# S5 tiles and state space heads in pairs, each of a pair in its own group of the array, and the first phases of S5 made at once

## The chip, the core and the metric

The kernel runs on one core of a Trainium2 chip. The metric is the time of one execution on the device in microseconds (us); lower is better. The core's engines are TensorE (PE), VectorE (DVE), ScalarE (ACT), GpSimd (POOL) and SyncE (SP), which issues the DMAs.

## The reference

Two blocks of layers run over one sequence of 256 positions with 2048 features, in f32. The change touches two pieces of them. The first is the state space layer (`ssd_scan`), with 64 heads of 64 columns in 8 groups and two chunks of 128 positions:

```python
decay = jnp.exp(jnp.where(causal, da_t[..., :, None] - da_t[..., None, :], -jnp.inf))
cb = jnp.einsum('bclgn,bcsgn->bcgls', cm, bm)
y_diag = jnp.einsum('bcgls,bcgels,bcsgep->bclgep', cb, decay, xdt)
```

The second is the S5 branch, a complex linear recurrence with 64 groups of 64 states, 16 inputs and 16 outputs each:

```python
x_r = jnp.einsum('bsgc,gpc->bsgp', ug, bb_r)
x_i = jnp.einsum('bsgc,gpc->bsgp', ug, bb_i)
_, _, h_r, h_i = lax.associative_scan(_complex_affine_combine, (a_seq_r, a_seq_i, x_r, x_i), axis=1)
y = (jnp.einsum('bsgp,gcp->bsgc', h_r, c_re) - jnp.einsum('bsgp,gcp->bsgc', h_i, c_im))
y = y + d_skip.reshape(N_SSM_GROUPS, SSM_GROUP) * ug
z = jax.nn.gelu(y.reshape(bsz, seq, D_SSM)) @ w_glu
```

Around them stand projections, an LRU and an mLSTM layer, gated linear attention, differential attention, gates and a feed-forward layer. Nearly all of the arithmetic is in products with 550 MB of weights.

## The kernel before

**The main stream.** All weight blocks of 128x128 come in a fixed order, eight to a unit, 1010 units. SP loads a unit into one of 7 RAW buffers (L2005), ACT copies it rounded into WH (L901), DVE forms the rest WL = RAW - WH (L1329), and PE makes three fp32r matmuls with each block: high and low weights by the high part of x, high weights by the low part. In most stages a matmul has 256 columns. WH has 5 buffers, so ACT waits for PE's last use of a unit, and the pace of all engines is PE's.

**The steps.** Everything else runs in chains of numbered steps beside the stream. `walk` goes through the plan on every engine alike: after each unit it runs one step of every open chain. So a step takes one unit, and the order of instructions in each engine's queue is written by the step numbers: what PE is to use at step r must be made by DVE or POOL in an earlier one, or PE stands in front of it with the main stream queued behind. `STEPS` holds the number of steps of each chain.

**State space heads.** In each group g of eight heads, `ssd(g, s)` has ACT make the decay DB of one head at each step 1 to 8 (L1089 ff.; it reads a row of running sums that a DMA has spread into CSB), DVE mask it at steps 2 to 9 (name "msk"), and PE multiply it at steps 3 to 10: two f32 products per head (256 and 128 columns, 64 weight columns XDT), into rows 0 to 63 of a bank for an even head and 64 to 127 for an odd one. DB has 3 buffers.

**S5.** 128 states (two groups) are a tile; there are 32 tiles. `s5_tiles` gives tile n the steps r = s - (11 + 11 (n // 2) + 5 (n % 2)), so two tiles take 11 steps. At r = 0 PE forms Bu (BR, BI: 32 rows of the array, by the tile's place n % 4), at 1 ACT copies it to BX and, swapped, to BS; at 2 DVE multiplies BX by the cosine table and POOL BS by the sine table (name "bsm"); at 3 DVE adds them, runs two scans into BS and multiplies by the cosine into HH, and POOL multiplies by the sine into BX ("bss"); at 5 DVE joins HH; at 6 PE forms y with CR and CI (32 columns of the array, by n % 4, into bank 7). BX has two buffers, BS and HH one. The odd tile's y stands in the same step as the even Bu of the next pair.

**Phases.** The tables TB (cosine and sine of the phase at 256 positions, two tiles a table, two tables) are made by POOL in `phases(b, r)` at steps 11 b + r, r = 0 to 8: each step doubles the length filled so far (for 64 positions and more by 64 at a time) in six operations, after the tile's own operations of the same step. The S5 chain runs beside the projections for gated attention (`gla`, `dec`), differential attention (`diff`) and the branch outputs (`g12`, `gb`, `db`). Its last steps apply GELU and split the result into ZS (`rest`); `End("s5")` runs what is left of it after the first tile of `g0`.

## Time and profile before

| | us |
|---|---|
| median of 3 runs | 3366.08 |
| lowest, highest | 3359.88, 3367.69 |
| the profiled execution | 3367.36 |
| its span in the trace | 3365.6 |
| PE busy, DVE busy | 3195.7, 2287.2 |
| ACT busy, POOL busy | 1841.0, 674.8 |

The page shows one execution. A matmul's record is longer than its share of PE's time, since matmuls overlap; the distance from start to start tells what one costs, and the idle time before an instruction what was waited for. [...]

### The profile page before, as it was taken

How to read it: one execution, taken by the hardware profiler on the slowest of the kernel's cores; microseconds unless marked ns; L12 is line 12 of the kernel's file. 1: busy time of each engine (PE TensorE's matmuls, PEld its weight loads, DVE VectorE, ACT ScalarE, POOL GpSimd, SP SyncE). 2: the span in 40 equal slices, each digit the busy share in tenths (PEclk: the TensorE clock that was granted, in tenths of full speed). 3: DMA queues.
4: the chain of work that ended last, by engine and by line, in shares of the span. 5: the costliest groups of instructions: out<-in, count | busy, mean ns of one | idle time of the engine just before them, and what ended most of it. 6: DMA issues, size and time to landing. Idle time of an engine off the chain costs nothing.

```text
span 3365.6 us, 54085 instructions
## 1 busy us (share of the span) xinstructions
PE 3195.7 (95%) x21726; PEld 2917.0 (87%) x21726; DVE 2287.2 (68%) x3156; ACT 1841.0 (55%) x2371; POOL 674.8 (20%) x1110
## 2 busy tenths in 40 slices
PE   6989898999999999998999998989999999999998
PEld 6889888889999999887887887888998888888887
DVE  6655788656778777656656676666566788888554
ACT  5544778545666666553555544333545666666443
POOL 1000000000000000114656777774001000000000
PEclk9999999999999999999999999889999999999999
DMA  5445444555455555555333433434555555555554
GB/s 195 145 132 178 137 149 153 195 191 197 169 170 174 170 171 191 179 180 192 132 113 117 134 126 127 137 126 146 205 183 187 188 191 191 188 192 190 188 191 140
DMA packets 158045, 560.53 MB, mean 167 GB/s; under 512 B 17552, under 2 KB 25808, under 8 KB 157152
## 3 DMA queue, kind: packets, MB, share of 16 engines
q1 hardware_dynamic: 157792, 557.06, 49.3%
q8 instruction: 170, 2.79, 0.3%
q14 instruction: 83, 0.68, 0.1%
HBM read 550.64 MB, written 6.36 MB: 165 GB/s over the span
## 4 chain that ended last, share of the span: by engine, by line
PE 70%; DVE 11%; POOL 8%; ACT 7%; issue 3%; DMA 1%; SPq 0%; DVEq 0%; ACTq 0%; POOLq 0%
PE ps L561 70%; POOL TB L1917 4%; DVE WL L1329 3%; ACT WH L901 2%; ACT L891 2%; POOL PT L1917 2%; POOL BX L1917 1%; POOL BS L1917 1%; DVE HH L1292 1%; DVE X L1303 0%; DMA scratch<-X 0%; DVE BS L1319 0%; DVE XC L1303 0%; DVE XV L1303 0%; DVE XC L1319 0%
## 5 line engine op out<-in xcount | busy, mean ns | idle before, releaser
L561 PE MATMUL ps<-XN,WH 128*128 128x256 f32 (+1 forms) x8864 | 1876.7, 305 | 47.6 <-DVE WL L1329 25.7
L901 ACT ACTIVATE WH<-RAW 128x1024 fp32r<-128x1024 f32 x1010 | 1065.5, 1057 | 1266.7 <-PE ps L561 1232.8
L1329 DVE TENSOR_TENSOR WL<-RAW,WH 128x1024 fp32r<-128x1024 f32 x1010 | 1262.5, 1256 | 499.4 <-ACT WH L901 492.8
L561 PEld LDWEIGHTS ps<-XN,WH 128*128 128x128 f32 x8864 | 1447.6, 194 | 137.8 <-DVE WL L1329 28.5
L561 PE MATMUL ps<-XN,WL 128*128 128x256 f32 x5120 | 1453.8, 284 | 0.0
L561 PEld LDWEIGHTS ps<-XN,WL 128*128 128x128 f32 x5120 | 989.0, 193 | 0.0
L561 PE MATMUL ps<-YS,WH 128*128 128x512 f32 (+1 forms) x1088 | 369.9, 388 | 4.7 <-DVE YS L1292 2.2
L1917 POOL TENSOR_TENSOR RSB<-RSB,SQ 128x256 f32<-128x256 f32 x75 | 75.0, 1000 | 1212.4 <-ACT SQ L891 1211.2
L561 PE MATMUL ps<-YS,WL 128*128 128x256 f32 x1056 | 296.5, 281 | 0.0
L561 PEld LDWEIGHTS ps<-YS,WH 128*128 128x128 f32 x1088 | 202.8, 189 | 49.0 <-DVE YS L1292 2.5
L1917 POOL TENSOR_TENSOR SQ<-SQ 128x512 f32<-128x512 f32 (+1 forms) x24 | 33.1, 1378 | 1052.5 <-ACT SQ L891 1051.5
L561 PE MATMUL ps<-HS,WH 128*128 128x512 f32 x688 | 238.6, 392 | 0.0
L891 ACT ACT_TABLE_LOAD x154 | 197.6, 1283 | 8.7 <-PE ps L561 1.7
L561 PEld LDWEIGHTS ps<-YS,WL 128*128 128x128 f32 x1056 | 199.4, 189 | 0.0
L561 PE MATMUL ps<-HS,WL 128*128 128x256 f32 x688 | 192.7, 280 | 0.0
L561 PEld LDWEIGHTS ps<-HS,WH 128*128 128x128 f32 x688 | 129.2, 188 | 28.5
L1917 POOL TENSOR_TENSOR TB<-TB,PW 128x128 f32<-128x128 f32 (+6 forms) x288 | 148.7, 516 | 22.6
L1917 POOL TENSOR_TENSOR PT<-TB,PW 128x128 f32<-128x128 f32 (+6 forms) x288 | 144.1, 500 | 22.6
L1917 POOL TENSOR_TENSOR TB<-TB,PT 128x128 f32<-128x128 f32 (+6 forms) x288 | 140.7, 489 | 22.6
L561 PEld LDWEIGHTS ps<-HS,WL 128*128 128x128 f32 x688 | 129.3, 188 | 0.0
L561 PE MATMUL ps<-ZS,WH 128*128 128x256 f32 x512 | 91.0, 280 | 3.0 <-DVE ZS L1292 3.0
L1292 DVE TENSOR_TENSOR X<-X,ps 128x256 f32<-128x256 f32 x128 | 53.9, 421 | 56.5 <-PE ps L561 53.1
(328 smaller groups left out, 3438.1 us busy)
## 6 DMA issues: line engine op xcount, KB each, us to landing
RAW<-in_w SPq DMA_DIRECT2D x1010, 512.0 KB, 3.3
CSB<-sums SPq DMA_DIRECT2D x64, 128.0 KB, 3.7
scratch<-X SPq DMA_DIRECT2D x2, 2048.0 KB, 7.9
X<-scratch SPq DMA_DIRECT2D x2, 2048.0 KB, 7.8
X<-in_x SPq DMA_DIRECT2D x4, 512.0 KB, 7.6
X<-in_x SPq DMA_DIRECT2D x1, 2048.0 KB, 9.2
out<-X SPq DMA_DIRECT2D x4, 512.0 KB, 2.6
WIF<-in_w_if SPq DMA_DIRECT2D x1, 576.0 KB, 14.4
```

The lines of the kernel that those rows point to most:

```text
L561: return pe.e.matmul(dst, l, r, start=start, stop=stop, skip_group_check=True)
L891: act.e.activation(dst, src, f, bias=bias, scale=scale).then_inc(*act.one(*names))
L901: act.e.activation(WH[:, w % NH, :], RAW[:, w % NB, :], ACT.Copy).then_inc(*act.one(("wh", w)))
L1292: dve.e.tensor_tensor(dst, a, b, op).then_inc(*dve.one(*names))
L1329: dve.e.tensor_tensor(WL[:, w % NB, :], RAW[:, w % NB, :], WH[:, w % NH, :].bitcast(F32), SUB).then_inc(*dve.one(("wl", w)))
L1917: pool.e.tensor_tensor(dst, a, b, op).then_inc(*pool.one(*names))
```

## The change

- State space heads: PE takes two heads at steps 4, 6, 8 and 10 instead of one at each step 3 to 10. The two 256-column products come first, one for each half of the array's columns, then the two with 128. DB has 4 buffers for 3; CSB 4 for 5; RS3 is dropped for RS1.
- S5: `s5_pairs` runs both tiles of a pair together, a pair every 10 steps, and the chain has 178 steps for 197. PE forms Bu of both at r = 0 (into two banks) and y of both at r = 10, each alternating between the two tiles; ACT copies at 1 and 2; DVE's and POOL's operations for even and odd tile stand at neighbouring steps (see the diff). BS has two buffers, and the joined result stays in BS, without HH.
- Phases: POOL makes the first 16 positions of all 32 tiles at once at steps 0 to 3 (`rotate` on PB), and then a pair's table from a copy and four doublings, the last with 128 new positions at once.

```diff
-NCSB = 5
+NCSB = 4
...
-    "dv": 1, "dq": 1, "diff": 15, "g12": 1, "gb": 1, "db": 1, "g0": 1, "gg": 1, "gl": 2, "s5": 197, "wo": 1,
+    "dv": 1, "dq": 1, "diff": 15, "g12": 1, "gb": 1, "db": 1, "g0": 1, "gg": 1, "gl": 2, "s5": 178, "wo": 1,
...
-        DB = [m(f"DB{i}", 384) for i in range(3)]
+        DB = [m(f"DB{i}", 384) for i in range(4)]
         YB = v3(m("YB", 1024), 4)
-        RS3 = m("RS3", 256)
...
-        BS = v3(m("BS", 512), 2)
-        HH = v3(m("HH", 512), 2)
-        PT = m("PT", 2 * 64)
+        BS = [v3(m(f"BS{i}", 512), 2) for i in range(2)]
+        PT = m("PT", 256)
...
+        PB = m("PB", 2 * 32 * 16).rearrange("p (c n a) -> p c n a", c=2, n=32)
...
-                if 3 <= s <= 10:
-                    e_ = s - 3
+                if s in (4, 6, 8, 10):
+                    e_ = s - 4
                     if e_ % 4 == 0:
                         take("side", "yb", g, e_ // 4)
                         kept.add(holder_of("yb", g, e_ // 4))
                     b = PS[holder_of("yb", g, e_ // 4)]
-                    c, r, d = 256 * ((e_ % 4) // 2), 64 * (e_ % 2), DB[e_ % 3]
-                    pe.wait_ge(*at("msk", g, e_))
-                    mm(b[r:r + 64, c:c + 256], XDT[:, 0, 64 * e_:64 * e_ + 64], d[:, 0:256], True, False)
-                    mm(b[r:r + 64, c + 128:c + 256], XDT[:, 1, 64 * e_:64 * e_ + 64], d[:, 256:384], False,
-                       True).then_inc(*pe.one(("ymm", g, e_)))
+                    c = 256 * ((e_ % 4) // 2)
+                    pe.wait_ge(*at("msk", g, e_ + 1))
+                    two = [(64 * i, DB[(e_ + i) % 4], slice(64 * (e_ + i), 64 * (e_ + i) + 64)) for i in range(2)]
+                    for q, d, x in two:
+                        mm(b[q:q + 64, c:c + 256], XDT[:, 0, x], d[:, 0:256], True, False)
+                    for q, d, x in two:
+                        i = mm(b[q:q + 64, c + 128:c + 256], XDT[:, 1, x], d[:, 256:384], False, True)
+                    i.then_inc(*pe.one(("ymm", g, e_), ("ymm", g, e_ + 1)))
...
-                for n, r in s5_tiles(s):
-                    ft, q_ = n // 4, n % 4
-                    rows = slice(32 * q_, 32 * q_ + 32)
+                for m, r in s5_pairs(s):
+                    ft = m // 2
+                    pair = [(n, slice(32 * (n % 4), 32 * (n % 4) + 32)) for n in (2 * m, 2 * m + 1)]
                     if r == 0:
-                        b = take("side", "bu", n)
+                        b = [take("side", "bu", n) for n, _ in pair]
                         pe.wait_ge(*at("us", ft))
                         pe.wait_ge(*at("b1"))
                         pe.wait_ge(*at("b2"))
-                        mm(b[:, 0:256], BR[rows, ft, :], US[rows, ft, :])
-                        mm(b[:, 256:512], BI[rows, ft, :], US[rows, ft, :]).then_inc(*pe.one(("bu", n)))
-                    if r == 6:
-                        if q_ == 0:
+                        for c, src in ((slice(0, 256), BR), (slice(256, 512), BI)):
+                            for i, (n, rows) in enumerate(pair):
+                                x = mm(b[i][:, c], src[rows, ft, :], US[rows, ft, :])
+                        x.then_inc(*pe.one(("bu", 2 * m), ("bu", 2 * m + 1)))
+                    if r == 10:
+                        if m % 2 == 0:
                             take("y", "sy", ft)
                         b = PS[holder_of("sy", ft)]
-                        pe.wait_ge(*at("hh", n))
+                        pe.wait_ge(*at("hh", 2 * m + 1))
                         pe.wait_ge(*at("cc"))
-                        mm(b[rows, 0:256], CR[:, n, :], HH[:, 0, :], True, False)
-                        mm(b[rows, 0:256], CI[:, n, :], HH[:, 1, :], False, True).then_inc(*pe.one(("sy", n)))
+                        for c, src in enumerate((CR, CI)):
+                            for n, rows in pair:
+                                x = mm(b[rows, 0:256], src[:, n, :], BS[n % 2][:, c, :], c == 0, c == 1)
+                        x.then_inc(*pe.one(("sy", 2 * m), ("sy", 2 * m + 1)))
...
-                for n, r in s5_tiles(s):
-                    if r == 1:
-                        b = bank("bu", n)
+                for m, r in s5_pairs(s):
+                    if r in (1, 2):
+                        n = 2 * m + r - 1
+                        b, i = bank("bu", n), n % 2
                         act.wait_ge(*at("bu", n))
                         if n > 1:
-                            act.wait_ge(*at("hh", n - 2))
-                        if n:
-                            act.wait_ge(*at("hhc", n - 1))
-                            act.wait_ge(*at("bss", n - 1))
-                        fn(BX[n % 2], v3(b, 2), ACT.Copy)
-                        fn(BS[:, 0, :], b[:, 256:512], ACT.Copy)
-                        fn(BS[:, 1, :], b[:, 0:256], ACT.Copy, ("bx", n), ("free", "bu", n), scale=-1.0)
-                if s == 192:
+                            act.wait_ge(*at("sy", n - 2))
+                        fn(BX[i], v3(b, 2), ACT.Copy)
+                        fn(BS[i][:, 0, :], b[:, 256:512], ACT.Copy)
+                        fn(BS[i][:, 1, :], b[:, 0:256], ACT.Copy, ("bx", n), ("free", "bu", n), scale=-1.0)
...
-                for n, r in s5_tiles(s):
-                    ft, q_ = n // 4, n % 4
-                    tb = TB[:, (n // 2) % 2]
-                    cc, ss = tb[:, 0, n % 2, :], tb[:, 1, n % 2, :]
-                    c2 = cc.unsqueeze(1).to_broadcast([128, 2, 256])
-                    b = BX[n % 2]
-                    if r == 2:
+                for m, r in s5_pairs(s):
+                    n = 2 * m + {2: 0, 3: 1, 4: 0, 5: 1, 7: 0, 8: 1}.get(r, 0)
+                    x, y = BX[n % 2], BS[n % 2]
+                    c2 = TB[:, m % 2, 0, n % 2, :].unsqueeze(1).to_broadcast([128, 2, 256])
+                    if r in (2, 3):
                         dve.wait_ge(*at("bx", n))
-                        dve.wait_ge(*at("tb", n // 2))
-                        tt(b, b, c2, MUL)
-                    if r == 3:
+                        dve.wait_ge(*at("tb", m))
+                        tt(x, x, c2, MUL)
+                    if r in (4, 5):
                         dve.wait_ge(*at("bsm", n))
-                        tt(b, b, BS, ADD)
+                        tt(x, x, y, ADD)
                         mg = MAG[:, n:n + 1].to_broadcast([128, 256])
                         for c in range(2):
-                            scan(BS[:, c, :], mg, b[:, c, :], 0.0, MUL, ADD, ("scn", n))
-                        if n:
-                            dve.wait_ge(*at("sy", n - 1))
-                        tt(HH, BS, c2, MUL, ("hhc", n))
-                    if r == 5:
+                            scan(y[:, c, :], mg, x[:, c, :], 0.0, MUL, ADD, ("scn", n))
+                    if r in (7, 8):
                         dve.wait_ge(*at("bss", n))
-                        tt(HH[:, 0, :], HH[:, 0, :], b[:, 0, :], SUB)
-                        tt(HH[:, 1, :], HH[:, 1, :], b[:, 1, :], ADD, ("hh", n))
-                    if r == 7 and q_ == 3:
-                        dve.wait_ge(*at("sy", n))
+                        tt(y, y, c2, MUL, ("hhc", n))
+                        tt(y[:, 0, :], y[:, 0, :], x[:, 0, :], SUB)
+                        tt(y[:, 1, :], y[:, 1, :], x[:, 1, :], ADD, ("hh", n))
+                    if r == 12 and m % 2:
+                        ft = m // 2
+                        dve.wait_ge(*at("sy", 2 * m + 1))
...
+            def rotate(tb, n, l, tiles, *names):
+
+                d = 1 << l
+                c, s_ = [PW[:, i, l, tiles].unsqueeze(2).to_broadcast([128, n, d]) for i in range(2)]
+                t = PT[:, 0:n * d].rearrange("p (n a) -> p n a", n=n)
+                x, y = slice(0, d), slice(d, 2 * d)
+                tt(tb[:, 0, :, y], tb[:, 0, :, x], c, MUL)
+                tt(t, tb[:, 1, :, x], s_, MUL)
+                tt(tb[:, 0, :, y], tb[:, 0, :, y], t, SUB)
+                tt(tb[:, 1, :, y], tb[:, 0, :, x], s_, MUL)
+                tt(t, tb[:, 1, :, x], c, MUL)
+                tt(tb[:, 1, :, y], tb[:, 1, :, y], t, ADD, *names)
...
+                    fill(PB[:, 0, :, 0:1], 1.0)
+                    fill(PB[:, 1, :, 0:1], 0.0)
+                if s < 4:
+                    rotate(PB, 32, s, slice(0, 32))
+                m, r = divmod(s - 4, 10)
+                if s >= 4 and m < 16 and r in (0, 1, 2, 4):
+                    tb = TB[:, m % 2]
+                    if r == 0:
+                        if m > 1:
+                            pool.wait_ge(*at("hhc", 2 * m - 3))
+                        pool.wait_ge(*pool.last)
+                        pool.e.tensor_copy(tb[:, :, :, 0:16], PB[:, :, 2 * m:2 * m + 2, :]).then_inc(*pool.one())
+                    rotate(tb, 2, {0: 4, 1: 5, 2: 6, 4: 7}[r], slice(2 * m, 2 * m + 2), ("tb", m))
+                for m, r in s5_pairs(s):
+                    n = 2 * m + {2: 0, 3: 1, 5: 0, 6: 1}.get(r, 0)
+                    x, y = BX[n % 2], BS[n % 2]
+                    ss = TB[:, m % 2, 1, n % 2, :]
+                    if r in (2, 3):
                         pool.wait_ge(*at("bx", n))
-                        tt(BS, BS, ss.unsqueeze(1).to_broadcast([128, 2, 256]), MUL, ("bsm", n))
-                    if r == 3:
+                        tt(y, y, ss.unsqueeze(1).to_broadcast([128, 2, 256]), MUL, ("bsm", n))
+                    if r in (5, 6):
                         pool.wait_ge(*at("scn", n))
-                        tt(b[:, 0, :], BS[:, 1, :], ss, MUL)
-                        tt(b[:, 1, :], BS[:, 0, :], ss, MUL, ("bss", n))
-                b, r = divmod(s, 11)
-                if b < 16 and r < 9:
-                    phases(b, r)
+                        tt(x[:, 0, :], y[:, 1, :], ss, MUL)
+                        tt(x[:, 1, :], y[:, 0, :], ss, MUL, ("bss", n))
...
+def s5_pairs(s):
+
+    return [(m, s - 9 - 10 * m) for m in range(16) if 0 <= s - 9 - 10 * m < 13]
```

On PE in the first group of heads the names are ps (bank), DB (decay of a head), XDT (weights of a head), XN, WH and WL (the main stream). Before, one unit of the main stream (cut here) stands between two heads:

```order
L561 MATMUL ps1<-XN_52,WL_50 128x256
L561 MATMUL ps5<-DB0_121,XDT_119 64x256
L561 MATMUL ps5<-DB0_121,XDT_119 64x128
L561 MATMUL ps2<-XN_52,WH_51 128x256 x2
...
L561 MATMUL ps2<-XN_52,WL_50 128x256
L561 MATMUL ps5<-DB1_122,XDT_119 64x256
L561 MATMUL ps5<-DB1_122,XDT_119 64x128
```

After, at the second of these two places:

```order
L560 MATMUL ps2<-XN_52,WL_50 128x256
L560 MATMUL ps5<-DB0_121,XDT_119 64x256
L560 MATMUL ps5<-DB1_122,XDT_119 64x256
L560 MATMUL ps5<-DB0_121,XDT_119 64x128
L560 MATMUL ps5<-DB1_122,XDT_119 64x128
```

The first head's products moved behind the unit that followed them, and the two heads alternate.

On PE in the later part of S5 (HH, or BS after, is the state; CR and CI form y in bank 7; US, BR and BI form Bu), before, at the step that holds the odd y and the next even Bu:

```order
L561 MATMUL ps7<-HH_162,CR_156 32x256
L561 MATMUL ps7<-HH_162,CI_157 32x256
L561 MATMUL ps6<-US_158,BR_154 128x256
L561 MATMUL ps6<-US_158,BI_155 128x256
```

After, where y of a pair and Bu of the next meet:

```order
L560 MATMUL ps7<-BS0_160,CR_155 32x256
L560 MATMUL ps7<-BS1_161,CR_155 32x256
L560 MATMUL ps7<-BS0_160,CI_156 32x256
L560 MATMUL ps7<-BS1_161,CI_156 32x256
L560 MATMUL ps6<-US_157,BR_153 128x256
L560 MATMUL ps3<-US_157,BR_153 128x256
L560 MATMUL ps6<-US_157,BI_154 128x256
L560 MATMUL ps3<-US_157,BI_154 128x256
```

All eight products of a pair's steps stand together; the two other places of S5 per pair are gone from PE.

On POOL in the same part (BS<-BS,TB is "bsm", BX<-BS,TB "bss", the rest phases), before, for an odd tile:

```order
L1917 TENSOR_TENSOR BS<-BS,TB 128x512
L1917 TENSOR_TENSOR TB<-TB,PW 128x2x64
L1917 TENSOR_TENSOR PT<-TB,PW 128x128
L1917 TENSOR_TENSOR TB<-TB,PT 128x2x64
L1917 TENSOR_TENSOR TB<-TB,PW 128x2x64
L1917 TENSOR_TENSOR PT<-TB,PW 128x128
L1917 TENSOR_TENSOR TB<-TB,PT 128x2x64
L1917 TENSOR_TENSOR BX_160<-BS,TB 128x256 x2
```

After, for both tiles of a pair:

```order
L1915 TENSOR_TENSOR BS_160<-BS_160,TB 128x512
L1915 TENSOR_TENSOR BS_161<-BS_161,TB 128x512
L1975 COPY TB<-PB 128x4x16
L1915 TENSOR_TENSOR TB<-TB,PW 128x2x16
...
L1915 TENSOR_TENSOR BX_158<-BS_160,TB 128x256 x2
L1915 TENSOR_TENSOR TB<-TB,PW 128x2x32
...
L1915 TENSOR_TENSOR BX_159<-BS_161,TB 128x256 x2
L1915 TENSOR_TENSOR TB<-TB,PW 128x2x64
```

The widest phases moved behind the last of a pair's products; six of 128x2x16 and six of 128x2x32 (or their PT form) stand before the even and the odd BX.

## Rows read from the trace of the kernel before

**Rows 1.** Page: the span, and PE's busy us, share and instructions.

```profile
span 3365.6 us, 54085 instructions
PE 3195.7 (95%) x21726; PEld 2917.0 (87%) x21726; DVE 2287.2 (68%) x3156; ACT 1841.0 (55%) x2371; POOL 674.8 (20%) x1110
```

**Rows 2.** Windows: stretch, length, busy us by engine, then PEclk, DMA share, GB/s.

```profile
820.00:1340.00 520.00, 517.45 (x3974) 483.69 (x3974) 392.32 (x557) 347.49 (x442) 19.30 (x14) 1.00 0.52 174
1600.00:2040.00 440.00, 406.35 (x2614) 358.89 (x2612) 293.98 (x419) 227.16 (x325) 301.40 (x557) 0.94 0.37 123
2040.00:2318.00 278.00, 252.75 (x1798) 231.65 (x1798) 175.91 (x218) 100.34 (x122) 208.54 (x362) 0.90 0.40 133
2600.00:3100.00 500.00, 500.00 (x2886) 437.31 (x2885) 405.75 (x612) 317.13 (x445) 6.64 (x7) 1.00 0.57 190
```

**Rows 3.** PE's waits, 2040 to 2318: releaser, us, times, longest.

```profile
PE ps L561 <- DVE HH L1292: 25.2, 6, 5.1
```

**Rows 4.** PE's waits, 1600 to 2040.

```profile
PE ps L561 <- DVE HH L1292: 14.8, 8, 4.2
PE ps L561 <- ACT RS L891: 6.6, 2, 4.1
```

**Rows 5.** Timeline of PE at a late y: start, us, instruction, idle before.

```profile
2121.04 0.62 PE L561 MATMUL ps<-HH,CR 128*32 128x256 f32 x2 [3.78 <-DVE HH L1292]
...
2124.45 0.41 PE L561 MATMUL ps<-DOS,WL 128*128 128x256 f32 x1
```

**Rows 6.** Timeline of POOL before that y.

```profile
2111.02 1.29 POOL L1917 TENSOR_TENSOR BS<-BS,TB 128x512 f32<-128x512 f32 x1
...
2115.73 1.26 POOL L1917 TENSOR_TENSOR PT<-TB,PW 128x128 f32<-128x128 f32 x1
2117.07 0.45 POOL L1917 TENSOR_TENSOR TB<-TB,PT 128x128 f32<-128x128 f32 x1
2117.66 2.32 POOL L1917 TENSOR_TENSOR BX<-BS,TB 128x256 f32<-128x256 f32 x2
```

**Rows 7.** Windows: one pair of S5 tiles, from Bu to Bu.

```profile
2140.51:2184.66 44.15, 40.43 (x282) 36.81 (x281) 28.28 (x36) 15.44 (x19) 34.70 (x63) 0.88 0.40 132
```

**Rows 8.** Groups of POOL, 1590 to 2345: count, busy us, mean ns, idle before.

```profile
L1917 POOL TENSOR_TENSOR BX<-BS,TB 128x256 f32<-128x256 f32 x64 | 72.9, 1139 | 54.0 <-DVE BS L1319 48.8
L1917 POOL TENSOR_TENSOR PT<-TB,PW 128x128 f32<-128x128 f32 x90 | 63.0, 699 | 7.1
...
L1917 POOL TENSOR_TENSOR TB<-TB,PW 128x64 f32<-128x64 f32 x30 | 14.6, 487 | 2.3
```

**Rows 9.** Timeline of PE around an undisturbed Bu, then y.

```profile
2097.48 0.28 PE L561 MATMUL ps<-XN,WL 128*128 128x256 f32 x1
...
2098.74 0.50 PE L561 MATMUL ps<-XN,WH 128*128 128x256 f32 x2
...
2101.60 0.28 PE L561 MATMUL ps<-XN,WL 128*128 128x256 f32 x1
2101.81 0.62 PE L561 MATMUL ps<-HH,CR 128*32 128x256 f32 x2
2102.26 0.59 PE L561 MATMUL ps<-HH,CI 128*32 128x256 f32 x2
2102.79 0.50 PE L561 MATMUL ps<-XN,WH 128*128 128x256 f32 x2
```

**Rows 10.** Timeline of PE: before the second head of a group, and the sixth.

```profile
834.07 0.28 PE L561 MATMUL ps<-XN,WL 128*128 128x256 f32 x1
...
849.49 0.28 PE L561 MATMUL ps<-XN,WL 128*128 128x256 f32 x1
850.13 0.86 PE L561 MATMUL ps<-DB,XDT 128*64 128x256 f32 x4 [0.36 <-DVE DB L1292]
```

**Rows 11.** PE's waits, 815 to 1345.

```profile
PE ps L561 <- DVE DB L1292: 2.5, 7, 0.4
```

**Rows 12.** Page: the costliest groups, the first products of ZS.

```profile
L561 PE MATMUL ps<-ZS,WH 128*128 128x256 f32 x512 | 91.0, 280 | 3.0 <-DVE ZS L1292 3.0
```

57 lines of the change are left out of this document (11 added, 46 removed).

## The prediction

> **What bounds the kernel now.** I read five views in this order. The page gives the span and TensorE (PE) at 95% busy [rows 1], so only PE's own work, PE's waits and PE's clock can move the time. The windows by stage then part the span [rows 2]. The state space stage (820 to 1340 us) has a granted clock of 1.00 and PE busy 517.45 of 520 us: PE alone bounds it. The feed-forward stage is PE-bound too, with VectorE (DVE) at 405.75 of 500 us, so a DVE share of 81% does not by itself hold PE up. The S5 stretch is different. [...] The list of PE's waits names one cause for the second part: six waits for the tile HH from DVE, 25.2 us [rows 3]. In the first part the same wait has 14.8 us, next to others [rows 4].
>
> The timeline shows what the wait is. Of each pair of S5 tiles the odd one is late: PE stands 3.78 us before the HH product, and the matmuls behind it are slow: one of 128x256 takes 0.41 us [rows 5] where it takes 0.28 at full clock [rows 9]. [...] The late part comes to 25.2 us of waits and (1 - 0.90) x 278 = 27.8 us of clock, together 53.0.
>
> Who is late is in GpSimd's (POOL's) timeline [rows 6]: the product BS (step 2 of a tile) begins at 2111.02, DVE's sum waits for it, and between it and the products BX (step 3) stand six phase operations, 2112.39 to 2117.5, one of them 1.26 us. BX begins at 2117.66, and HH follows only at 2120. POOL was busy 34.70 of 44.15 us in the next pair's window, with some 0.08 us between operations (63 x 0.08 = 5): 39.7 of 44.15 [rows 7]. It is nearly full, in an order that puts phases ahead of what PE waits for.
>
> **The change, part by part.**
>
> 1. POOL's phases. Before, each pair costs 54 phase operations. After, the first sixteen phases of all 32 tiles are made once (24 operations and two fills), and a pair costs one copy and 24 operations of 128x32, 128x64, 128x128 and 128x256. By the means of the S5 stretch [rows 8]: the twelve narrow ones at the 0.49 us of a 128x64, 5.9; six of 128x128 at 0.69, 4.1; six of 128x256, a shape the phases do not have now, bounded by the 1.14 of BX (6.8) and by two 128x128 (8.3), and I take 6.8, the same shape; two BS at the 1.29 of [rows 6], 2.6; four BX at 1.14, 4.6; the copy 0.5. That is 24.5, with 31 gaps of 0.08 27.0 us a pair. The table made at once is about 6 x (0.49 + 0.49 + 0.69 + 1.14) = 16.9 us, before the first tile needs POOL, where POOL now makes 54 operations for the first pair: nothing.
>
> 2. The steps. A pair now takes 10 units of eight blocks instead of 11, BS has two steps before DVE's sum instead of one, and HH two between DVE and PE instead of one (DVE at steps 7 and 8, PE at 10). The odd BS is followed by copy and six 128x32 and then the even BX, so what stands ahead of a waited-for product is 3.4 us instead of the 5.1 from 2112.39 to 2117.5. PE's own time for 10 units: a unit is 24 matmuls 0.12 apart, 2.87 us, so 28.7 plus the packed products below, 31.5. POOL needs 27.0 of it, DVE 28.28 of 44.15 now [rows 7], about 26.8 with one unit less: 85%, a little over the feed-forward's 81%. Everything fits, PE is the longest, and what is late next is the odd HH again, by the least slack. I leave 1 us per pair for it in the six late pairs (6 us) and count the rest as won: 53.0 - 6 = **47 us**. Bounds: 26 (half stays) to 53.
>
> 3. The early part (1600 to 2040). [...] But PE also waits there for ACT and DVE in chains of gated attention and differential attention [rows 4], which start at PE's own products; a PE that comes earlier waits longer there, and S5's steps, moved by up to 19 units, now meet other steps in the queues of ACT and DVE. Bounds 0 and 32 us. I take the lower end, **0**.
>
> 4. Products in different groups of the array. Each f32 product is two halves on PE, 0.22 us apart for 256 columns (2101.81 to 2102.26 holds two) [rows 9]. A group of four halves costs start to start, less one ordinary 0.12, 1.14 us for Bu and 1.07 for y [rows 9], and 0.1 more on leaving, since the second matmul after it is late. For a state space head four units take 849.49 - 834.07 = 15.42 us, 3.86 each [rows 10]: 0.99 above 2.87. No row shows two products in different groups one behind the other, so this is bounded from both sides. One after another, only a lead-in per pair goes: four halves more cost 0.88, so Bu 2.12 against 2 x 1.24, y 2.05 against 2 x 1.17, heads 1.65 against 2 x 0.99; 0.65 x 16 + 0.33 x 32 = 21 us. Entirely side by side: half of all, (1.24 + 1.17) x 16 + 0.99 x 32 = 70 us. The order of issue lies between: the two halves of one product share a group, and PE starts in order, so only the second half of one and the first of the next can overlap, at three borders of seven. That gives Bu 2.12 - 0.66 = 1.46, y 1.39, heads 1.65 - 0.44 = 1.21 (the borders at 128 columns are half as wide): **31.5 us** in S5 and (1.98 - 1.21) x 32 = 24.6 in the heads. A dearer exchange of groups (0.1 at each of three borders, 64 pairs) would take 19 us off the 21 of the lower bound.
>
> [...]
>
> 5. The heads' own waits. One head of a group is late today: PE idles 0.36 us at 850.13 [rows 10], seven times, 2.5 us in all [rows 11]. It is the sixth. Now PE comes to it without the fifth's 0.99 us, whose product is moved behind the same wait, so it waits 0.99 longer: 7 x 0.99 = 6.9. ACT's copies have four buffers for three, CSB four for five; a row lands long before its use. The heads give 24.6 - 6.9 = **17.7 us** (bounds 4 and 25).
>
> 6. The end. S5 is done 19 units before the gated sums need ZS, and that wait of **3.0 us** goes [rows 12].
>
> Two side banks are taken at once for Bu where one was; ACT frees them in the next two steps, before the four of the ring come round, and I count nothing.
>
> Sum: 47 + 0 + 31.5 + 17.7 + 3.0 = 99 us. The profiled execution took 3367.4 us (span 3365.6), so 3268; the median of the runs is 1.3 lower. I forecast **3267 us**.
>
> **The rivals.**
> - No overlap of groups at all: the products give 21 instead of 56, so 3267 + 35 = 3302 us. For it: no row shows overlap. Chance 0.13.
> - Rows overlap, columns don't: y loses 0.66 x 16 = 10.6 and the heads 0.44 x 32 = 14, 3292 us. Chance 0.10.
> - The early part gives all its 32 us too: 3235 us. For it: four of its waits look exactly like the late ones. Against: the other waits in rows 4. Chance 0.11.
> - POOL and DVE hold each other up more than the means say, and half of the late stalls with their slow clock stay: 3267 + 26 = 3293 us. For it: a 128x128 product of POOL took 1.26 us beside DVE's split and 0.45 without [rows 6], and DVE's share rises to 85%. [...] Chance 0.10.
> - **Slower.** The same mechanism in full: each of POOL's 31 operations a pair waits for one of DVE's, as the 1.26 did, now that wide ones replace the narrow. At 1.40 us each the pair takes 46 us. S5 then takes 16 x 46 + 18 x 2.87 = 788 us, where it takes 741 now (1600 to 2341); less 20.7 for heads and end that is +26: 3392 us. It turns at 44.4 us a pair, against 27.0 by the means. Chance 0.03.
> - The pairs do nothing: the stall moves whole to the new waiting place, and groups do not overlap: of the 21 us and the 3 of ZS the heads' wait takes 6.9 and a dearer exchange of groups some 10: 3359 us. Chance 0.03.
>
> **How the numbers follow.** The forecast has 0.50, and its own range is 3250 to 3285. From 3235 to 3302 all rivals but the last two lie, 0.94 by the cases; full overlap alone lies at 3253, together with the early part at 3221. I widen only upward, to 3310, for clock and waits that none of the cases names. A difference under 0.3% (10 us) can't be told from no change in this kernel. Faster by more than that: all but the last two cases, 0.94; within it 0.03; slower 0.03.
>
> **What the profile after would show.** Step 2: PE's wait for its y product under 10 us in all and the granted clock of the last S5 pairs near 1.00, a pair every 31 to 33 us. Step 1: POOL busy some 25 us a pair. Step 3: new waits of PE for ACT or DVE in the attention part, as long as those of HH that went. Step 4: the starts of eight halves in one group, 1.4 us from first to leaving instead of 2. Step 5: a wait of 1.3 us at the third pair of heads of each group. The prediction is wrong if POOL's operations lengthen beside DVE, or if the eight halves start 0.22 apart.

## The result

| kernel | median of the runs, us | lowest to highest | profiled span, us |
|---|---|---|---|
| before | 3366.89 | 3359.88 to 3369.28 | 3365.6 |
| after | 3268.49 | 3265.13 to 3270.49 | 3268.7 |

The ratio is 0.971, with a 95% interval of 0.9698 to 0.9722: 98.4 us less. The forecast was 3267 us, so the sum came out within 2 us. Two of its terms did not: the products of S5 were 6 us too small, and the gain of the heads was about twice too large. The rest of this text takes them apart.

The page after begins with these two lines. They answer to [rows 1]: PE does the same 21726 instructions in 87 us less busy time, and POOL has 640 operations where it had 1110.

```profile
span 3268.7 us, 53596 instructions
PE 3108.3 (95%) x21726; PEld 2873.6 (88%) x21726; DVE 2313.3 (71%) x3156; ACT 1837.6 (56%) x2371; POOL 541.3 (17%) x640
```

The windows after, over the stretches of [rows 2] (stretch, length, busy us by engine, then PEclk, DMA share, GB/s). The stretches are the same times from the start, not the same work, since after runs ahead by then.

```profile
820.00:1340.00 520.00, 501.26 (x4005) 480.83 (x4004) 394.29 (x559) 348.16 (x444) 22.40 (x16) 0.98 0.55 176
...
1600.00:2040.00 440.00, 407.64 (x2836) 372.85 (x2835) 346.36 (x462) 238.73 (x341) 261.52 (x338) 0.95 0.40 133
2040.00:2318.00 278.00, 275.01 (x2299) 269.57 (x2298) 209.70 (x252) 129.61 (x151) 119.95 (x134) 1.00 0.55 182
```

PEclk is the mean granted clock of the stretch, as a share of full speed. The traces of all kernels here record two levels of it, 1.00 and 0.50, and the mean of a stretch with both lies between. Behind the late product of [rows 5] it is 0.50 from 2123 to 2129 us, and there the matmuls of 128x256 start 0.21 us apart (2124.66 to 2124.87), where they start 0.12 apart at 1.00 (832.43 to 832.55 in after).

Three readings. The late S5 stretch went from a granted clock of 0.90 to 1.00, and PE is busy 275 of 278 us there. The early stretch hardly moved, 0.94 to 0.95. And the state space stage, which was at 1.00 and full, is now at 0.98 and PE is idle for 19 of 520 us. That last row is the surprise of the profile: the change made PE's products there shorter, and PE began to wait.

PE's waits after, late stretch (2040 to 2260), then the state space stage (820 to 1345). They answer to [rows 3] and [rows 11].

```profile
PE ps L560 <- DVE BS L1293: 3.0, 3, 1.3
```

```profile
PE ps L560 <- DVE DB L1293: 18.7, 15, 2.3
```

The wait for HH (now in place, in BS) is 3.0 us instead of 25.2. The wait for DB is 18.7 us instead of 2.5.

PE's timeline where both products of two S5 tiles follow each other (x4 is four halves, two products), then at a pair of heads (x8 is eight halves). Records overlap: that of a matmul of the main stream is 0.28 us long, with 0.12 us from its start to the next, so starts are compared.

```profile
2067.51 0.28 PE L560 MATMUL ps<-XN,WL 128*128 128x256 f32 x1
2067.72 0.63 PE L560 MATMUL ps<-BS,CR 128*32 128x256 f32 x4
2068.17 0.60 PE L560 MATMUL ps<-BS,CI 128*32 128x256 f32 x4
2068.70 0.70 PE L560 MATMUL ps<-US,BR 32*128 32x256 f32 x4
2069.24 0.60 PE L560 MATMUL ps<-US,BI 32*128 32x256 f32 x4
2069.77 0.50 PE L560 MATMUL ps<-GOS,WH 128*128 128x256 f32 x2
```

```profile
832.76 0.87 PE L560 MATMUL ps<-DB,XDT 128*64 128x256 f32 x8
833.56 0.50 PE L560 MATMUL ps<-XN,WH 128*128 128x256 f32 x2
```

In [rows 9] two halves of CR took 0.45 us from start to start (2101.81 to 2102.26). Here four of them do (2067.72 to 2068.17). Two halves of BR took 0.54 in before (2097.69 to 2098.22), and four do here (2068.70 to 2069.24). The head product took 0.86 with four halves [rows 10], and eight take 0.87. The second member of each pair adds 0.01 us at most, in products that differ in rows (Bu) and in products that differ in columns (y, heads).

### The profile page after: what moved, and what is told of

It reads as the page before. It is cut to its first block, busy times and chain, and to the rows that moved or that the text cites. A ratio compares the mean times of both kernels' runs of the same rounds, so it can differ in the third digit from the quotient of the medians.

```text
span 3268.7 us, 53596 instructions
## 1 busy us (share of the span) xinstructions
PE 3108.3 (95%) x21726; PEld 2873.6 (88%) x21726; DVE 2313.3 (71%) x3156; ACT 1837.6 (56%) x2371; POOL 541.3 (17%) x640
## 4 chain that ended last, share of the span: by engine, by line
PE 75%; DVE 11%; ACT 8%; issue 2%; POOL 1%; DMA 1%; SPq 0%; DVEq 0%; ACTq 0%; POOLq 0%
PE ps L560 75%; DVE WL L1330 3%; ACT WH L907 2%; ACT L897 2%; DVE XV L1304 1%; DVE BS L1293 1%; POOL TB L1915 1%; DMA scratch<-X 0%; DVE X L1304 0%; ACT DB L897 0%; DVE BS L1320 0%; DVE XC L1304 0%; DVE XMC L1304 0%; DMA RAW<-in_w 0%; ACT RB L897 0%
## 5 line engine op out<-in xcount | busy, mean ns | idle before, releaser
L1915 POOL TENSOR_TENSOR TB<-TB,PT 128x32 f32<-128x32 f32 (+3 forms) x128 | 99.6, 778 | 10.0
L1304 DVE SCALAR_TENSOR_TENSOR VG<-UP,CV,VG 128x256 f32<-128x256 f32 x172 | 83.3, 484 | 12.6 <-DVE HS L1293 0.5
L560 PE MATMUL ps<-MS,WH 128*128 128x512 f32 x256 | 88.9, 392 | 0.9 <-DVE DVT L1293 0.9
```

What stands on the lines that cost most here:

```text
L560: return pe.e.matmul(dst, l, r, start=start, stop=stop, skip_group_check=True)
L1304: dve.e.scalar_tensor_tensor(out=dst, in0=a, scalar=s, in1=b, op0=o0, op1=o1).then_inc(*dve.one(*names))
L1915: pool.e.tensor_tensor(dst, a, b, op).then_inc(*pool.one(*names))
```

## The experiments

All times are medians. Each kernel was run in turn with the kernel before, whose median was 3368.07 in the first series, 3368.01 in the second and 3366.23 in the last.

| kernel | us | ratio to before, 95% interval |
|---|---|---|
| e1_heads_only | 3359.81 | 0.9971 (0.9962 to 0.9981) |
| e2_same_group | 3301.94 | 0.9802 (0.9787 to 0.9817) |
| e3_one_by_one | 3268.50 | 0.9703 (0.9690 to 0.9717) |
| e4_silu_late | 3247.43 | 0.9642 (0.9629 to 0.9655) |
| e5_short_phases | 3310.43 | 0.9828 (0.9815 to 0.9842) |
| e6_long_phases | 3310.44 | 0.9829 (0.9816 to 0.9843) |
| e7_unit_later | 3241.99 | 0.9628 (0.9614 to 0.9641) |
| e8_before_silu_late | 3365.31 | 0.9987 (0.9978 to 0.9996) |
| e9_s5_only | 3278.81 | 0.9736 (0.9720 to 0.9753) |

### Do different groups overlap, and does the order count?

**e2_same_group.** The kernel after, with the same number and size of matmuls, but both members of a pair in one group.

```diff
-                    c = 256 * ((e_ % 4) // 2)
...
-                    two = [(64 * i, DB[(e_ + i) % 4], slice(64 * (e_ + i), 64 * (e_ + i) + 64)) for i in range(2)]
-                    for q, d, x in two:
+                    q = 64 * ((e_ % 4) // 2)
+                    two = [(256 * i, DB[(e_ + i) % 4], slice(64 * (e_ + i), 64 * (e_ + i) + 64)) for i in range(2)]
+                    for c, d, x in two:
...
-                                x = mm(b[i][:, c], src[rows, ft, :], US[rows, ft, :])
+                                x = mm(b[i][:, c], src[pair[0][1], ft, :], US[pair[0][1], ft, :])
...
-                                x = mm(b[rows, 0:256], src[:, n, :], BS[n % 2][:, c, :], c == 0, c == 1)
+                                x = mm(b[pair[0][1], 256 * (n % 2):256 * (n % 2) + 256], src[:, n, :], BS[n % 2][:, c, :], c == 0, c == 1)
```

It computes something else: the products of the odd tiles and of half of the heads are left out or misplaced, so only its time says something.

> The kernel after, with both members of a pair in the same group of the array: Bu of an odd tile takes the rows of the even one, y of both lands in the even tile's partitions in two column ranges, and two heads of a pair land in the same 64 partitions in two column ranges (so the odd tiles' products are left out or misplaced; number, size and order of the matmuls are the same). If different groups are what overlaps, eight halves take 0.88 us more in Bu and in y (the 0.22 per half of the rows before): 0.88 x 2 x 16 = 28 us in S5, and 0.44 to 0.66 per pair of heads, which mostly shortens a wait that is there anyway: 3292 to 3305. If the saving came from packing eight halves behind one wait (one lead-in instead of two) and not from the groups, the time stays within 5 us of 3268.

Measured: 3301.94 us, 33.4 more than after. PE's timeline in it, at the same two places:

```profile
2061.40 1.05 PE L560 MATMUL ps<-BS,CR 128*32 128x256 f32 x4
2062.28 1.03 PE L560 MATMUL ps<-BS,CI 128*32 128x256 f32 x4
2063.24 1.13 PE L560 MATMUL ps<-US,BR 32*128 32x256 f32 x4
2064.21 1.02 PE L560 MATMUL ps<-US,BI 32*128 32x256 f32 x4
2065.16 0.50 PE L560 MATMUL ps<-DOS,WH 128*128 128x256 f32 x2
```

```profile
834.25 1.51 PE L560 MATMUL ps<-DB,XDT 128*64 128x256 f32 x8
835.70 0.51 PE L560 MATMUL ps<-XN,WH 128*128 128x256 f32 x2
```

From the first CR to the matmul behind BI it is now 3.76 us, and 2.05 in after (2067.72 to 2069.77): 1.71 more, x 16 pairs = 27.4 us. The four rows grow nearly alike, by 0.43, 0.43, 0.43 and 0.42 from start to start, so rows and columns overlap equally well. The groups are what overlaps; that the pair shares one wait and one lead-in is not enough. The other 6 us fit the heads: by the two rows a pair costs 0.64 more (1.51 for 0.87), 20 us for 32 pairs, while the stage's granted clock is 1.00 instead of 0.98 (10.5 us less) and its waits are 4.9 us shorter, 13.8 instead of 18.7:

```profile
PE ps L560 <- DVE DB L1293: 13.8, 14, 1.7
```

**e3_one_by_one.** The kernel after, with all products of the first tile or head issued ahead of those of the second.

```diff
-                        for c, src in enumerate((CR, CI)):
-                            for n, rows in pair:
+                        for n, rows in pair:
+                            for c, src in enumerate((CR, CI)):
```

and likewise for Bu and the heads.

> The kernel after, with the pair's products issued one tile (or head) after the other, all of the first and then all of the second, instead of alternating. By the prediction's step 4 only the second half of one product and the first of the next can overlap, so now one border of seven is left where three were: 0.44 us more for each eight halves against the step's own value, and against the full overlap that the trace shows 0.66 more in Bu and y, 0.66 x 32 = 21 us in S5, 3285 to 3292 (the heads' part hides in their wait). If PE starts products of another group ahead of the queue, whatever the order, nothing changes: 3264 to 3272.

Measured: 3268.50 us, the time of after to 0.01 us. Its timeline of PE:

```profile
2067.79 0.63 PE L560 MATMUL ps<-BS,CR 128*32 128x256 f32 x4
2068.25 0.61 PE L560 MATMUL ps<-BS,CI 128*32 128x256 f32 x4
2068.78 0.71 PE L560 MATMUL ps<-US,BR 32*128 32x256 f32 x4
```

The program has CR, CI of one tile and then CR, CI of the other. The trace has all four halves of CR start first. So the second tile's first product starts beside the first tile's, ahead of a product that stands before it in the queue. By the start times of the single halves it begins 13 ns after the first tile's (2067.790 and 2067.803); in after, where it stands next in the queue, 7 ns (2067.717 and 2067.724). The prediction's rule (PE starts in order, so only borders between neighbours overlap) was its author's estimate. In [rows 9] CR, CI and WH do start in the order of the queue, at 2101.81, 2102.26 and 2102.79, but no row has two products in different groups. The rule falls with this run: within such a group of eight halves the order does not count.

### Where did the heads' gain go?

**e1_heads_only.** The kernel before, with the heads' part of the change alone.

```diff
-NCSB = 5
+NCSB = 4
...
-        DB = [m(f"DB{i}", 384) for i in range(3)]
+        DB = [m(f"DB{i}", 384) for i in range(4)]
...
-                if 3 <= s <= 10:
-                    e_ = s - 3
+                if s in (4, 6, 8, 10):
+                    e_ = s - 4
```

> The kernel before with the heads' part of the change alone: heads two by two, four buffers DB and CSB, nothing of S5. The prediction on record says 17.7 us less than before (24.6 from the products, 6.9 lost in a new wait), 3349. What the two traces say together: by the last group of the state space stage the changed kernel is only 2.4 us ahead and by the end of the output projection about 7, so this part should give 3 to 8 us, 3359 to 3364, with waits for DB near 19 us in all and a granted clock of about 0.97 in the stage. A third view, that the heads' part pays but S5's steps took it back, would give 15 us or more here.

Measured: 3359.81 us, 8.3 less than before (6 to 13 by the interval). It waits as after does, in 820 to 1345:

```profile
PE ps L560 <- DVE DB L1292: 18.8, 15, 2.3
```

So the loss belongs to this part of the change, not to S5. The chain is in after's timeline of ACT at the middle of a group's heads (columns: start, us, instruction, idle before):

```profile
837.93 1.28 ACT L897 ACT_TABLE_LOAD   x1
839.22 1.06 ACT L897 ACTIVATE ZB<-ZB 128x1024 f32<-128x1024 f32 x1
840.37 0.95 ACT L897 ACTIVATE DB<-CSB,CST 128x256 f32<-128x256 f32 x2
841.34 1.28 ACT L897 ACT_TABLE_LOAD   x1
842.63 0.52 ACT L897 ACTIVATE DB<-DB 128x384 f32<-128x384 f32 x1
```

then DVE's and PE's:

```profile
843.19 0.56 DVE L1293 TENSOR_TENSOR DB<-DB,CBm 128x384 f32<-128x384 f32 x1 [4.08 <-ACT DB L897]
...
848.01 0.56 DVE L1293 TENSOR_TENSOR DB<-DB,CBm 128x384 f32<-128x384 f32 x1
```

```profile
848.62 1.55 PE L560 MATMUL ps<-DB,XDT 128*64 128x256 f32 x8 [2.31 <-DVE DB L1293]
...
850.69 0.41 PE L560 MATMUL ps<-XN,WL 128*128 128x256 f32 x1
```

ACT changes its table for the Silu of the z tiles and changes back for the next exponential: 1.28 + 1.06 + 1.28 us in the middle of the heads. DVE stands 4.08 us for it. By the time it has done that mask, a split, a row of the next group's convolution and the next mask, PE has waited 2.31 us for the sixth head, and runs the eight halves in 1.55 instead of 0.87 and the matmuls behind them at 0.41 instead of 0.28: the granted clock is 0.50 from 849 to 851 us.

**e4_silu_late.** The kernel after, with that Silu behind the last head.

```diff
-            def zs(g, j, s):
-                if j == 3:
-                    act.wait_ge(*at("zsr", g))
-                    fn(ZB, ZB, ACT.Silu, ("zsd_", g))
...
                     fn(d, d, ACT.Exp, ("dec_", g, e_), scale=-1.0)
+                if s == 9:
+                    act.wait_ge(*at("zsr", g))
+                    fn(ZB, ZB, ACT.Silu, ("zsd_", g))
```

> The kernel after, with ACT's Silu of the four z tiles moved from the middle of a group's heads (step of the fourth z tile) to step 9 of the group, behind the last head's exponential. Reading of the trace: that Silu with two loads of tables, 1.28 us each, is what makes the fifth and sixth heads' DB late, so PE waits about 2.6 us per group and then runs some 2 us worth of time at 1.2 GHz; without it the waits for DB fall from 18.7 to under 5 us, the granted clock of the stage to 1.00, and the time by 7 x 4.5 = 31 us, to 3235 to 3245. The rival: what is late is DVE, which has a row of the next group's convolution (4 operations, 2.4 us) between two masks; then the Silu gives only what ACT saves, under 8 us, 3260 or more.

Measured: 3247.43 us, 21.1 less than after. The waits and the window of 820 to 1345:

```profile
PE ps L560 <- DVE DB L1291: 4.5, 14, 0.3
```

```profile
820.00:1345.00 525.00, 518.37 (x4153) 495.37 (x4153) 414.09 (x584) 359.22 (x462) 29.07 (x22) 1.00 0.58 184
```

The waits shrink by 14.2 us and the clock returns to 1.00, which is worth about 0.02 x 525 = 10.5 us; together 24.7. The expectation of 31 multiplied the worst group by seven; the total of the list of waits, with the clock, comes within 4 us of what was measured. No run shows the clock in GHz that the expectation names; what after shows in that spell is the granted clock of 0.50. That the Silu in the middle makes PE wait is shown, and the rival (DVE's convolution row alone is late) is out.

**e8_before_silu_late.** The same edit of the Silu, made in the kernel before.

> The kernel before, with the Silu of the z tiles moved behind the last head alone. There PE waits only 2.5 us in all for the heads and its clock in the stage is 1.00, so by the reading of the traces this gives 2.5 us or less, 3364 to 3368: the Silu in the middle of the heads costs nothing until PE's products are shorter. If it gives 10 us or more, the gain of e4_silu_late had nothing to do with the change.

Measured: 3365.31 us, 2.7 less than before (1 to 7 by the interval), and the list of waits for DB is empty. The Silu in the middle cost about 3 us while the products were long, and 21 once they were short.

**e9_s5_only.** The kernel after without the heads' part.

```diff
-                if s in (4, 6, 8, 10):
-                    e_ = s - 4
+                if 3 <= s <= 10:
+                    e_ = s - 3
```

> The kernel after, with the heads' part taken back: heads one by one, three DB and five CSB, everything of S5 as changed. The heads' part alone gave 8 us (e1_heads_only); if the two parts do not touch each other this one has the rest, 3268.5 + 8 = 3276 us, within 3 us, with a granted clock of 1.00 in the state space stage. By the prediction on record it would be 3267 + 17.7 = 3285.

Measured: 3278.81 us, 87.4 less than its before, 10.3 more than after, with a clock of 1.00 in the stage:

```profile
820.00:1345.00 525.00, 522.45 (x4008) 488.18 (x4007) 395.13 (x559) 349.08 (x444) 22.36 (x16) 1.00 0.52 175
```

The two parts add up within the intervals: 87.4 + 8.3 = 95.7 against 98.4.

### Phases or steps?

**e5_short_phases.** The kernel before, its steps and single tiles untouched, with the phases of the change.

```diff
-                b, r = divmod(s, 11)
-                if b < 16 and r < 9:
-                    phases(b, r)
+                if s == 0:
+                    ...
+                    for l in range(4):
+                        rotate(PB, 32, l, slice(0, 32))
+                b, r = divmod(s, 11)
+                if b < 16 and r in (0, 1, 2, 4):
+                    ...
+                    rotate(tb, 2, {0: 4, 1: 5, 2: 6, 4: 7}[r], slice(2 * b, 2 * b + 2), ("tb", b))
```

> The kernel before, with GpSimd's phases of the change alone: the first sixteen phases of all tiles made once, then a copy and four doublings per pair of tiles (steps 0, 1, 2 and 4 of eleven). Tiles one by one, their steps and the heads stay as before. If the load and the order of GpSimd's queue were the cause of the late HH (step 1 of the prediction), the waits for HH in the late stretch fall from 25.2 to under 8 us, the granted clock there from 0.90 to 0.97 or more, and the time by 40 to 50 us, to 3318 to 3328. If the missing slack was in the steps (one step between BS, the sum, BX and HH), phases alone give half or less: 3340 or more.

Measured: 3310.43 us, 57.6 less than before. Its waits of PE from 2040 to 2290, and the windows of one late pair of tiles and of both stretches:

```profile
PE ps L562 <- DVE HH L1293: 2.7, 4, 0.9
```

```profile
2129.77:2165.89 36.12, 36.12 (x283) 33.69 (x281) 29.25 (x36) 15.68 (x19) 25.73 (x31) 1.00 0.50 162
1600.00:2040.00 440.00, 414.82 (x2764) 370.24 (x2763) 321.74 (x436) 237.64 (x338) 220.62 (x289) 0.97 0.40 130
2040.00:2290.00 250.00, 247.27 (x1928) 230.87 (x1927) 196.58 (x235) 105.92 (x128) 148.33 (x170) 1.00 0.49 159
```

The late stalls are gone with the old steps, so GpSimd's phases were their cause. Two things changed in its queue at once, the load and the order: no phase stands any more between the odd tile's BS and its BX, where [rows 6] had six.

```profile
2154.51 1.56 POOL L1918 TENSOR_TENSOR BS<-BS,TB 128x512 f32<-128x512 f32 x1
2160.38 2.93 POOL L1918 TENSOR_TENSOR BX<-BS,TB 128x256 f32<-128x256 f32 x2 [4.31 <-DVE BS L1320]
```

Which of the two would have been enough is not shown; no kernel was timed with all the phases and only their order changed. The early stretch improves too, from a clock of 0.94 to 0.97 and from 14.8 to 10.1 us of waits for HH (0.03 x 440 = 13 and 4.7 us), which covers what came beyond the 40 to 50 us expected.

**e6_long_phases.** The kernel after, with eight doublings per pair.

```diff
-                m, r = divmod(s - 4, 10)
-                if s >= 4 and m < 16 and r in (0, 1, 2, 4):
+                m, r = divmod(s - 2, 10)
+                if s >= 2 and m < 16 and r < 8:
...
-                    rotate(tb, 2, {0: 4, 1: 5, 2: 6, 4: 7}[r], slice(2 * m, 2 * m + 2), ("tb", m))
+                    rotate(tb, 2, r, slice(2 * m, 2 * m + 2), ("tb", m))
```

> The kernel after, with the phases of each pair made from the start again, by eight doublings in eight steps (48 operations and two fills per pair instead of 24 and a copy); pairs, steps and heads stay as changed. By the load: the pair of after has 26.9 us of GpSimd's work and some 2.6 of gaps; 24 narrow operations at 0.49 + 0.08 add 13.7, so about 43 us a pair against the 30.9 that PE takes. Then GpSimd bounds the late pairs, 8 to 16 of them by 12 us: 3365 to 3460. If the steps and pairs alone removed the stalls, the time stays under 3290.

Measured: 3310.44 us, 42.0 more than after, neither of the two expectations. PE's waits from 2040 to 2330 and the window of a late pair:

```profile
PE ps L560 <- DVE BS L1293: 21.7, 5, 7.8
```

```profile
2116.84:2155.03 38.19, 33.92 (x258) 31.85 (x257) 26.31 (x33) 15.34 (x19) 33.52 (x57) 0.91 0.41 138
```

The late pairs take 38 to 43 us, as the load says, and POOL is busy 33.52 of 38.19. But only four pairs start late enough to feel it. I had priced 8 to 16. In the early stretch the ten units hold the products of the attention parts as well, and a pair takes 30 to 57 us in after anyway (the first Bu of the pairs at 1593.36, 1623.52, 1665.62, 1722.49, 1758.54); POOL's 40 us mostly fit. In this kernel, then, the price of a full GpSimd is paid only where PE has nothing beside it.

Together with before and after these two make a square: phases alone -57.6, everything but the phases -57.6, both -99.5 (3368.0 to 3268.5). It is a square only nearly, since e6's phases are not quite those of before: 48 operations a pair for 54, at other steps. The sum of the single effects is 15.7 us larger than the whole. Most of that lies in the early stretch (step 3 below), the rest in late stalls that go with either.

### How much hangs on the position in the attention parts?

**e7_unit_later.** e4_silu_late with all steps of S5 one unit later.

```diff
-    return [(m, s - 9 - 10 * m) for m in range(16) if 0 <= s - 9 - 10 * m < 13]
+    return [(m, s - 10 - 10 * m) for m in range(16) if 0 <= s - 10 - 10 * m < 13]
```

> The kernel e4_silu_late, with all of S5 (phases, tiles and its end) one unit later. In the late stretch PE is busy throughout, so nothing changes there. If what is left between 1500 and 2040 us (some 30 us of waits and 20 of clock) comes from S5 steps that fall upon steps of the attention parts in the queues of ACT and DVE, another position moves it by 5 to 15 us either way from 3247; if it comes from chains of the attention parts alone, the time stays within 3 us of 3247.

Measured: 3241.99 us (3241.27 to 3243.82) against 3247.43 (3246.84 to 3248.35) of e4_silu_late. The 95% intervals of the two ratios overlap a little, the runs do not. The early stretch of e4_silu_late and then of e7_unit_later:

```profile
1600.00:2040.00 440.00, 407.61 (x2838) 372.84 (x2838) 345.82 (x461) 238.41 (x342) 262.82 (x336) 0.95 0.40 131
```

```profile
1600.00:2040.00 440.00, 406.09 (x2879) 371.58 (x2879) 352.28 (x466) 240.74 (x344) 268.69 (x342) 0.97 0.41 134
```

That is 5.4 us for one unit, and the granted clock of the stretch goes from 0.95 to 0.97. Position matters there, by about the least that was expected. This is the fastest kernel of the study, 3.7% faster than before and 0.8% faster than after. Other positions were not timed.

## Why the sum was right, and its terms were not

| step | gain forecast, us | gain measured, us | from |
|---|---|---|---|
| late stalls | 47 | 46 to 50 | unit by unit; waits 25.2 to 3.0 and clock 0.90 to 1.00 over 278 us |
| early stretch | 0 | about 3 | unit by unit, 1500 to 2040 us |
| S5's products | 31.5 | 37.4 | pair of e5 against pair of after |
| heads | 17.7 | 7 to 10.3 | unit by unit 6.9; e1_heads_only 8.3; after against e9_s5_only 10.3 |
| wait for ZS | 3.0 | 3.0 | page, below |
| sum | 99 | 98.4 | medians |

"Unit by unit" is a comparison of the same work instead of the same times: the same matmul of the main stream is looked up in both traces. After is 0.6 us ahead of before at 818 us of before's time, 5.9 at 1338, 7.5 at 1498, 29.1 at 2040, 93.3 at 2340 and 96.6 at 2406. Some 19 of the 37.4 us of shorter products fall before 2040, by the number of Bu and y issued until then, which leaves 21.6 - 19 = 3 us for the rest of the early stretch and 64.2 - 18.5 = 46 for the late stalls.

**Step 1, POOL's load: right.** By the means of the S5 stretch a pair costs POOL 25 us, forecast at 24.5. The window of a late pair has 26.88; it holds 33 operations, two more than a pair has:

```profile
2129.63:2161.80 32.17, 30.84 (x258) 29.65 (x257) 28.55 (x35) 14.62 (x18) 26.88 (x33) 1.00 0.51 164
```

The same row has DVE busy 28.55 us, 89% of the pair against the 85% forecast, and PE still has the longest share. Of the uncertain sizes, the groups of POOL from 1600 to 2320 show the wide phases at or under the 1.14 that was taken, the 128x32 at 0.52 for 0.49, and the 128x64 at 0.65 to 0.74 for the same 0.49:

```profile
L1915 POOL TENSOR_TENSOR TB<-TB,PT 128x256 f32<-128x256 f32 x30 | 33.0, 1102 | 2.4
L1915 POOL TENSOR_TENSOR PT<-TB,PW 128x256 f32<-128x256 f32 x30 | 28.6, 955 | 2.3
...
L1915 POOL TENSOR_TENSOR PT<-TB,PW 128x64 f32<-128x64 f32 x30 | 22.3, 743 | 2.4
...
L1915 POOL TENSOR_TENSOR TB<-TB,PT 128x32 f32<-128x32 f32 x30 | 15.6, 522 | 2.3
```

**Step 2, the late stalls: right in size, one cause too many.** 53.0 less the 3.0 us that are left is 50, where 6 us were kept back, and unit by unit it is 46. But I credited the phases and the new steps together. e5 shows that the phases suffice: with the old steps the late waits are 2.7 us and the clock is 1.00, and unit by unit e5 gains 45 us there. What the shorter period and the new steps add in the late stretch is not to be told from nothing. The rival in which POOL and DVE hold each other up did not come about, though both are busier than forecast. The row given for it was read wrongly. The 0.45 us in [rows 6] belongs to another operation (TB from TB and PT), and a split of DVE began while it ran. The same operation as the one of 1.26 us, with DVE idle, is this one, so the contrast holds, with 0.40 for 0.45. The rows show the longer time beside DVE's split, not what an operation of POOL waits for in it:

```profile
2109.93 0.40 POOL L1917 TENSOR_TENSOR PT<-TB,PW 128x128 f32<-128x128 f32 x1
```

**Step 3, the early stretch: right within 3 us, but as a difference.** In the same stretch after has these waits of PE, where [rows 4] had HH with 14.8:

```profile
PE ps L809 <- DVE GE L1293: 5.6, 2, 4.8
PE ps L560 <- ACT RS L897: 4.9, 2, 2.4
PE ps L560 <- DVE BS L1293: 4.7, 2, 3.4
...
PE ps L560 <- DVE ST L1304: 3.0, 1, 3.0
```

The waits for HH went from 14.8 to 4.7, and GE and ST, which were no waits before, took 8.6 us. From 1340 to 2040 all waits of PE come to 52.4 us before and 51.5 after. That is the exchange of one wait for another that was forecast. What the forecast did not see is that the phases alone do help here: unit by unit e5 is 17 us ahead of before by 2040, of which after, without its shorter products, keeps 3. So the new steps give back some 14, and one unit of position is worth 5 (e7). No run shows the 32 us of the upper bound: 14.8 of it are the waits of [rows 4], the rest was the author's estimate of slow clock behind them. The runs showed 10.1 us less of these waits in after, 0.01 x 440 = 4.4 us of clock, and about 3 us in all. One term counted as nothing was not: between 1500 and 1600 after loses 3.9 us of its lead, and e5 2.5, which both make the table of all tiles there; e6, without it, loses 1.1. Nothing but this comparison says that the table is the cause.

**Step 4, the products: the rule was wrong, in the cautious direction.** It allowed an overlap at three borders of seven. The groups overlap entirely, within what the starts can tell: eight halves take 0.98 us (y, 2067.72 to 2068.70) and 1.07 (Bu, to 2069.77) where some 1.4 were forecast. Where PE never waits, a pair takes 36.12 us in eleven units in e5, 4.55 above 11 x 2.87, and in after 30.91 in ten (2036.60 to 2067.51), 2.21 above 28.7: 2.34 x 16 = 37.4 us, near the upper bound of 38.6. For the heads, two single ones take 2 x 0.99 above their units and a pair 1.00 (starts at 1035.66 and 1042.40 in after, 6.74 for two units of 2.87): 0.98 x 32 = 31.4 us, against 24.6. The second rival, in which rows overlap and columns don't, would make y and the heads dearer than Bu. The trace does not agree: y's four halves take 0.45 from start to start, Bu's 0.54, both as long as two did.

**Step 5, the heads' wait: the term that failed.** The place was right, the third pair of each group. The size was not: 0.99 us longer was forecast, and the waits rose by 16.2 us in all, 2.3 per group. Two things were missed. First, PE saves more ahead of that wait than the fifth head's product: 2 x 0.98 us on the two pairs before it as well, 2.95 in all. The wait grew from 0.36 to 2.31, so 1.95 of the 2.95 turned into waiting; and the fourth pair waits too. Second, idle time cost clock: 0.02 x 525 = 10.5 us at the state space stage. 31.4 - 16.2 - 10.5 leaves 4.7 by the rows, against 7 to 10 by the units and the runs. One group shows it: over the ten units that hold the first group's heads before needs 37.03 us (824.82 to 861.85), after 36.91 (824.27 to 861.18) and e4 33.49 (824.48 to 857.97). Of the 3.9 us that four pairs save, after keeps 0.1 and e4 3.5. The view that would have told it was there: the idle 0.36 of [rows 10] means that no slack is left, and every saving ahead of it had to be tested against the same chain. In e2 the waits for DB are 13.8 us, the longest 1.7, and the clock of the stage is 1.00; whether it is the length of the single wait that decides was not separated from the rest.

**Step 6, ZS: right.** The page after has no idle time before these products:

```profile
L560 PE MATMUL ps<-ZS,WH 128*128 128x256 f32 x512 | 90.9, 280 | 0.0
```

In e5, which has the old steps, the 3.0 us are there still.

So S5's products gave 5.9 us more than forecast, the early stretch about 3 more, the late stalls between 1 less and 3 more, and the heads 7 to 11 less, and the errors cancel. The cause of the late stalls was right; that the sum came within 2 us is luck. The single terms are not safe to carry on: the one for the heads hid the 21 us that one moved Silu brings.

## What to carry to other kernels

Small products that fill only part of the array are worth pairing in different row or column groups: here the second one added 0.01 us or less (0.45 us for y and 0.54 for Bu, alone or paired, 0.87 against 0.86 for heads), and their order in the queue needed no care (3268.50 us against 3268.49). When an engine is made faster between two waits for the same chain, count the saving only up to the slack at the wait, then look on the chain for something that can move, such as a function that changes ACT's table twice (here 2 x 1.28 us around a Silu of 1.06). Where one engine's queue is nearly full (POOL here, 39.7 of 44.15 us), try the lighter queue by itself first: here the new steps added nothing in the late stretch that could be measured on top of it. And compare two traces at the same work, not at the same time, before splitting a gain into terms.

## What the hardware showed that was not expected

- Eight halves of f32 products in two groups take the time of four: 0.87 us against 0.86 for heads (columns), and 0.45 against 0.88 for four halves of y in different and in one group. In y of after the halves of one tile start at 2067.717 and 2067.957 us and those of the other 7 ns behind each of them.
- PE starts matmuls of the other group ahead of ones queued before them in the first group (e3_one_by_one), at least within eight halves: 13 ns after the first half, where the second half of the same product starts 0.24 us after it. Deeper queues and four groups at once were not tried.
- One wait of 2.3 us per group of 67.7 us in an otherwise full stage went with a fall of the granted clock from 1.00 to 0.98 there, and a spell of matmuls at 0.41 us where 0.28 is usual. Without the wait (e4) the stage is at 1.00.
